# Down-projection weights in 8 KB runs, expert activations with even and odd features apart

## The chip, the core and the metric

The kernel runs on one core of one Trainium2 chip. The metric is the device time of one execution in microseconds (us), as the median of several runs. The core has five instruction streams that matter here: TensorE (PE, the matrix multiplies, with PEld for its weight loads), VectorE (DVE), ScalarE (ACT), GpSimd (POOL) and SyncE (SP, which in this kernel issues nearly all DMA transfers). Sixteen DMA engines carry the transfers between the chip's HBM and the on-chip SBUF.

## What is computed

One decoder layer on 256 tokens of width 1024, in float32: three token mixers (block-sparse attention, short convolution, cross-attention), then a routed feed-forward part with 32 experts, then a final RMSNorm. The change touches the experts alone. Each token goes to its four best experts. Cut to what matters, an expert computes:

```python
def expert_block(args):
    xb, e = args
    gu = xb @ w_gu[e] + b_gu[e]
    g = jnp.minimum(gu[:, :D_EXPERT], SWIGLU_LIMIT)
    lin = jnp.clip(gu[:, D_EXPERT:], -SWIGLU_LIMIT, SWIGLU_LIMIT)
    glu = g * jax.nn.sigmoid(SWIGLU_ALPHA * g)
    return ((lin + 1.0) * glu) @ w_down[e] + b_down[e]
```

`w_gu[e]` is 1024 x 2048 (8 MB), `w_down[e]` is 1024 x 1024 (4 MB). All 32 experts together hold 384 MB of weights, and each weight is read once.

## The kernel before

The kernel has two stages. The first, up to about 300 us, is the mixers: weights come in pieces of 1 MB into a ring of buffers. The second is the experts, one *step* per expert. In a step TensorE multiplies the expert's gathered tokens (64 slots) with `w_gu`, ScalarE and VectorE form the activations, TensorE transposes them and multiplies them with `w_down`, and the result is scattered back into accumulators in PSUM.

Weights of the experts arrive in pieces of 1024 KB (1.0486 MB as the profile counts), all issued by SP, in program order on one queue. `up_piece` (line 333) loads 128 rows of `w_gu` into one of the 16 slots of `ring`: partition p gets row p of the piece, 2048 floats, one run of 8 KB in HBM and in SBUF. Eight such pieces make an expert. `down_piece` (line 343) loads 256 rows of `w_down` into one of the four slots of `dring`: partition p gets rows p and p + 128 of the piece, each 1024 floats, that is two runs of 4 KB that lie 512 KB apart in HBM. Four such pieces make an expert, and `dring` holds just one expert's down weights.

SP waits before an up piece until TensorE has used what was in its slot (`pieces_used`), and before a down piece likewise (`downs_used`). For most of the experts it issues in the order up(e + 2), down(e + 1), up(e + 3), down(e + 2); the last eight experts (`IN_ORDER`) go up(e), down(e), and so the last transfers that TensorE needs are the up pieces of expert 31 and, behind them, its down pieces.

One step on the compute engines:

- TensorE, line 1245: 64 matmuls over the eight up pieces, with a wait for each piece; the gate half goes to `gate_ps` and the linear half to `lin_ps`. The 64 slots fill half of the array's columns, so that the features 0 to 511 sit in partitions 0 to 63 and the features 512 to 1023 in partitions 64 to 127, and `hid` is 128 x 512.
- VectorE, lines 940, 941, 944 and 947: `g_sb` = min(gate, 7), `hid` = clipped linear half, `hid` = (`hid` + 1) * `g_sb`, and last `hid` = `hid` * `sg`, where `sg` is ScalarE's sigmoid of `g_sb` (line 571). The last one sets `hid_ready`.
- TensorE meanwhile transposes the scatter matrix, gathers the next tokens (lines 1253, 1210, 1168), then waits for `hid_ready`, transposes `hid` in four blocks of 128 features (line 1265) into `gate_ps`, and ScalarE copies them to `hidT` (line 576).
- TensorE, line 1281: 32 matmuls with the four down pieces, with a wait for each piece (`down_in`), into `y_ps`. The k-th block of 128 rows is multiplied with the block of `hidT` that holds the same 128 features.

What orders the work is fixed in the code: each engine's program is a loop written by hand with semaphores between the engines.

Of the kernel before, what the change touches and what calls it, by code (L numbers as in the profile page):

```python
# [18 lines left out]
P = 128  # L19
# [95 lines left out]
def build(nc, a, out, scratch, ctx):  # L115
# [4 lines left out]
    ALU = mybir.AluOpType  # L120
# [20 lines left out]
    dring = region("dring", [P, DRING, PIECE])  # L141
# [20 lines left out]
    ident = consts[:, C_ID:C_ID + P]  # L162
# [59 lines left out]
    g_sb = region_r[:, 512:1024]  # L222
    sg = region_r[:, 1024:1536]
    hid = region_r[:, 1536:2048]
    hidT = region_r[:, 3072:3584]

    x2T = region_r[:, 0:2048].rearrange("p (c t) -> p c t", c=KC)
    logit_parts = region_r[:, 4096:4352]
# [19 lines left out]
    gate_ps, lin_ps, tr_ps, y_ps = bank[4], bank[5], bank[6], bank[7]  # L248
# [11 lines left out]
    down_in = [sem(f"down_in{n}") for n in range(DRING)]  # L260
# [23 lines left out]
    g_ready, up_read, hid_half, hid_ready = sem("g_ready"), sem("up_read"), sem("hid_half"), sem("hid_ready")  # L284
# [12 lines left out]
    def _(sp):  # L297
# [11 lines left out]
        p = 0  # L309
# [30 lines left out]
                up_piece(expert, slot0 + c, c)  # L340

        def down_piece(expert, j):
            sp.dma_start(dring[:, j, :].rearrange("p (c n) -> p c n", c=2),  # L343
                         a["w_down"][0, bass.ds(expert, 1), j * 256:(j + 1) * 256, :]
                         .rearrange("e (c p) n -> p (e c) n", p=P)).then_inc(down_in[j], 16)

        def expert_down(expert, uses):

# [34 lines left out]
        with sp.Fori(0, IN_ORDER) as i:  # L383
            for u in range(2):
                e = i * 2 + (e0 + u)
# [210 lines left out]
    def _(dve):  # L596
# [197 lines left out]
        for g in range(len(GROUPS)):  # L794
            p = N_PROJ + 3 * g
            for u in range(2):
                j = ATT_H + 2 * g + u
# [53 lines left out]
        for t in range(TT):  # L851
            last = dve.scalar_tensor_tensor(logit[:, t, :], bank[5][:, t * E:(t + 1) * E], norm[:, 2, 6 + t:7 + t], b_rt,
                                            ALU.mult, ALU.add)
# [7 lines left out]
        for k in range(TOPK):  # L861
            for t in range(TT):
                if k == 0:
                    last = dve.tensor_scalar(mask[:, t, :], slot_no[:, 0:E], best_i[:, t, 0:1], None, ALU.is_equal)
                else:
                    last = dve.scalar_tensor_tensor(mask[:, t, :], slot_no[:, 0:E], best_i[:, t, k:k + 1],
                                                    mask[:, t, :], ALU.is_equal, ALU.add)
# [49 lines left out]
        for t in range(TT):  # L917
            for b in range(PASSES):
                last = dve.tensor_scalar(wexp[:, t, b * E:(b + 1) * E], elog[:, t, :], small[:, 4 + t:5 + t], None, ALU.mult)
        dve.memset(wexp[:, :, STEPS:], 0.0)  # L920
        last = dve.memset(place[:, :, STEPS:], -1.0)
# [11 lines left out]
        with dve.Fori(0, more * (E // 4) + E // 4) as i:  # L933
            for u in range(4):
                s = i * 4 + u
                if u % 2 == 0:
                    dve.wait_ge(gathered, s + 2)
                    gather_matrices(s + 2)
                dve.wait_ge(pieces_used, (s + 1) * KC + N_MIX)
                dve.tensor_scalar(g_sb, gate_ps[:, :], LIMIT, None, ALU.min).then_inc(g_ready, 1)  # L940
                dve.tensor_scalar(hid, lin_ps[:, :], LIMIT, -LIMIT, ALU.min, ALU.max).then_inc(up_read, 1)  # L941
                dve.wait_ge(g_ready, s + 1)
                dve.wait_ge(up_read, s + 2)
                dve.scalar_tensor_tensor(hid, hid, 1.0, g_sb, ALU.add, ALU.mult).then_inc(hid_half, 1)  # L944
                dve.wait_ge(hid_half, s + 1)
                dve.wait_ge(sig_ready, s + 1)
                dve.tensor_tensor(hid, hid, sg, ALU.mult).then_inc(hid_ready, 1)  # L947
                dve.wait_ge(w_slot_ready, s + 1)
                dve.tensor_scalar(scaT[u % 2][:, :, :].rearrange("p t s -> p (t s)"), y_ps[:, 0:TT * P], 0.0, None,
                                  ALU.not_equal).then_inc(scaT_sb, 1)  # L950
                bias_selector(s + 1)
                dve.wait_ge(gathered, s + 3)
                gathered_half(tr_ps, (u // 2 + 1) % 2, u % 2)
                scatter_matrix(s + 1)

                dve.wait_ge(downs_used, (s + 1) * DRING)
                dve.wait_ge(y_high, s + 1)
                dve.scalar_tensor_tensor(y_parts[64:128, 0:512], y_ps[0:64, :], w_slot[0:64, :],  # L958
                                         y_parts[0:64, 0:512].bitcast(fp32), ALU.mult, ALU.subtract)
                dve.scalar_tensor_tensor(y_parts[0:64, 512:1024], y_ps[64:128, :], w_slot[64:128, :],  # L960
                                         y_parts[64:128, 512:1024].bitcast(fp32), ALU.mult, ALU.subtract)\
                    .then_inc(y_ready, 1)
# [3 lines left out]
        for t in range(TT):  # L966
# [6 lines left out]
            for half in range(2):  # L973
                cut = slice(half * 512, half * 512 + 512)
                last = dve.scalar_tensor_tensor(x2[:, t, cut], acc[t][half][:, :], at, gain_out[:, cut], ALU.mult, ALU.mult)
# [4 lines left out]
    def _(pe):  # L980
        mm, transpose = pe.matmul, pe.transpose
# [167 lines left out]
        for j in range(4):  # L1149
# [6 lines left out]
            for n, (k, t, half) in enumerate(order):  # L1156
                c = 2 * j + k
                last = product(bank[2 + 2 * t + half][:, :], (merged_high, merged_low), w,
                                              (slice(None), c, slice(t * P, (t + 1) * P)),
                                              (slice(None), k, slice(half * 512, half * 512 + 512)), c == 0, c == KC - 1)  # L1160
# [18 lines left out]
        for t in range(TT):  # L1179
            pe.wait_ge(x2T_sb if t else x2T_copied, 2)  # L1180
            for c in range(KC):
                at = 32 * (c % 4)
                last = mm(bank[4 - t][at:at + 32, 0:P], w_rt[:, c, :], x2T[:, c, t * P:(t + 1) * P],
                          start=(c < 4), stop=(c >= 4))
            last.then_inc(logit_parts_done, 1)

        for t in range(TT):
            pe.wait_ge(logit_parts_sb, t + 1)
            last = mm(bank[5][:, t * E:(t + 1) * E], logit_parts[:, t * P:(t + 1) * P], pick[:, 0:E], start=True, stop=True)
# [34 lines left out]
        for t in range(TT):  # L1224
            last = transpose(bank[7][0:E, t * P:(t + 1) * P], wexp[:, t, 0:E], ident)
# [6 lines left out]
        with pe.Fori(0, more * (E // 4) + E // 4) as i:  # L1232
            for u in range(4):
                s = i * 4 + u
                slot0 = 8 if u % 2 == 0 else 0

                pe.wait_ge(up_read, s + 1)
                bias_rows(0)
                for c in range(KC):
                    if u % 2 == 0 and c % 4 == 0:  # L1240
                        pe.wait_ge(xg_sb, s + 1 + c // 4)
                    pe.wait_ge(piece_in[slot0 + c], i * 32 + 16 * (u // 2) + 16 * (loads_before(slot0 + c) + 1))
                    for k, ps in enumerate((gate_ps, lin_ps)):
                        for half in range(2):
                            last = mm(ps[64 * half:64 * half + 64, :], xg[u // 2][:, c, 64 * (u % 2):64 * (u % 2) + 64],  # L1245
                                      ring[:, slot0 + c, k * F + half * 512:k * F + half * 512 + 512],
                                      start=False, stop=(c == KC - 1))
                    last.then_inc(pieces_used, 1)

                pe.wait_ge(y_ready, s + 1)  # L1250
                pe.wait_ge(sca_ready, s + 1)
                for t in range(TT):
                    last = transpose(y_ps[:, t * P:(t + 1) * P], sca[:, t, :], ident)
                last.then_inc(scaT_done, 1)

                pe.wait_ge(xg_sb, s + 2)
                if u % 2 == 0:
                    pe.wait_ge(gat_ready, i * 2 + (u // 2 + 2))
                gather(tr_ps, u % 2)
                pe.wait_ge(scaT_sb, s + 1)  # L1260
                scatter((u + 1) % 2, 0, False)

                pe.wait_ge(hid_ready, s + 1)
                for c in range(4):
                    last = transpose(gate_ps[:, c * P:(c + 1) * P], hid[:, c * P:(c + 1) * P], ident)  # L1265
                last.then_inc(hidT_done, 1)
                scatter((u + 1) % 2, 1, False)

                pe.wait_ge(up_read, s + 2)
                pe.wait_ge(sel_ready, s + 2)  # L1270
                bias_rows(1)
                pe.wait_ge(hidT_sb, s + 2)
                pe.wait_ge(scaT_sb, s + 2)
                pe.wait_ge(w_slot_ready, s + 1)
                for c in range(KC):
                    if c % 2 == 0:
                        pe.wait_ge(down_in[c // 2], (s + 1) * 16)
                    lhsT = hidT[:, (c % 4) * P + 64 * (c // 4):(c % 4) * P + 64 * (c // 4) + 64]
                    for half in range(2):
                        at = (c % 2) * D + half * 512  # L1280
                        last = mm(y_ps[64 * half:64 * half + 64, :], lhsT, dring[:, c // 2, at:at + 512],  # L1281
                                  start=(c == 0), stop=(c == KC - 1))
                    if c % 2:
                        last.then_inc(downs_used, 1)
# [45 lines left out]
```

## Time and profile before

| what | before |
|---|---|
| time, median of 3 runs | 1239.49 us (1239.25 to 1241.49) |
| time of the profiled execution | 1238.82 us |
| its span, first to last instruction | 1236.7 us |
| TensorE busy | 1130.2 us, 91% |
| VectorE busy | 387.2 us, 31% |
| ScalarE busy | 263.6 us, 21% |
| bytes moved by DMA | 452.08 MB |

The profiled execution lies 0.67 us below the median of the runs, and 2.1 us of it lie outside the span. A page of the profile shows the span in 40 slices with the busy share of each engine; views of the trace show single stretches: what each engine did, how many bytes the DMA engines moved and in packets of which size, and what an engine waited for. A busy TensorE is not TensorE at its peak, since its matmuls are pipelined and their ends are modelled.

### The profile page before, as it was taken

The page shows a single profiled execution, that of the slowest core. Times are in us where ns is not written, and L with a number is a line of the kernel's source. Part 1 is how long each engine was busy: PE and PEld are TensorE (multiplying, and loading weights), DVE is VectorE, ACT ScalarE, POOL GpSimd, SP SyncE. Part 2 cuts the span into 40 slices and gives each one's busy share as a digit, 9 for nine tenths or more (in the row PEclk, how much of TensorE's full clock was granted, in tenths as well). Part 3 has the DMA queues.
Part 4 walks back from the last instruction along what each step waited for, and adds up shares of the span by engine and source line. Part 5 has one row for each costly group of instructions (what it writes and reads, how often), then busy time and mean ns, then how long its engine had stood idle before and what let it go on. Part 6 is the DMA issues. An engine that isn't in the chain of part 4 may idle for free.

```text
span 1236.7 us, 15845 instructions
## 1 busy us (share of the span) xinstructions
PE 1130.2 (91%) x6083; PEld 583.4 (47%) x6083; DVE 387.2 (31%) x716; ACT 263.6 (21%) x403; POOL 8.3 (1%) x10
## 2 busy tenths in 40 slices
PE   5999999998999999889998889998898999988886
PEld 4999999995443333333333333333333333333332
DVE  6657655564231221212121212122222222221213
ACT  5334575442111110101010101010111111010102
POOL 2000000000000000000000000000000000000000
PEclk8999999999999999999999999999999999999999
DMA  7984344776999999999999999999999999999995
GB/s 261 346 270 160 125 166 140 290 282 250 420 418 417 418 418 418 417 418 417 418 418 418 418 418 418 417 419 417 417 417 417 411 418 418 417 418 418 418 418 224
DMA packets 109427, 452.08 MB, mean 366 GB/s; under 512 B 7074, under 2 KB 38039, under 8 KB 76631
## 3 DMA queue, kind: packets, MB, share of 16 engines
q1 hardware_dynamic: 108871, 449.95, 91.3%
q0 software_dynamic: 528, 1.73, 0.5%
q8 instruction: 21, 0.34, 0.1%
q14 instruction: 7, 0.06, 0.0%
HBM read 450.59 MB, written 1.06 MB: 365 GB/s over the span
## 4 chain that ended last, share of the span: by engine, by line
SPq 40%; PE 38%; DMA 15%; DVE 3%; issue 3%; ACT 0%; DVEq 0%; ACTq 0%
SPq L343 21%; PE bank L991 19%; SPq L333 18%; PE bank L1245 8%; DMA dring<-in_w_down_dram 8%; PE bank L1281 6%; DMA ring<-in_w_gu_dram 6%; DVE region_r L944 1%; DVE region_r L947 1%; DVE region_r L940 1%; PE bank L1265 1%; DVE region_r L941 0%; PE bank L1216 0%; PE bank L998 0%; DVE memT_low L636 0%
## 5 line engine op out<-in xcount | busy, mean ns | idle before, releaser
L1245 PE MATMUL bank<-ring,region_x 128*64 128x512 f32 x2048 | 452.7, 595 | 14.4 <-DMA ring<-in_w_gu_dram 14.4
L1281 PE MATMUL bank<-dring,region_r 128*64 128x512 f32 x1024 | 253.1, 637 | 56.1 <-DMA dring<-in_w_down_dram 55.1
L1245 PEld LDWEIGHTS bank<-ring,region_x 128*64 128x64 f32 x2048 | 141.7, 137 | 305.0 <-issue 263.7
L1281 PEld LDWEIGHTS bank<-dring,region_r 128*64 128x64 f32 x1024 | 71.3, 144 | 223.7 <-DMA dring<-in_w_down_dram 112.3
L940 DVE TENSOR_SCALAR region_r<-bank 128x512 f32<-128x512 f32 x32 | 22.1, 692 | 374.4 <-PE bank L1245 374.4
L958 DVE SCALAR_TENSOR_TENSOR y_parts<-bank,region_r,y_parts 64x512 fp32r<-64x512 f32 x32 | 23.8, 744 | 350.8 <-ACT y_parts L580 350.8
L571 ACT ACTIVATE region_r<-region_r 128x512 f32<-128x512 f32 x32 | 20.2, 630 | 439.3 <-DVE region_r L940 439.3
L991 PE MATMUL bank<-hT_high,w_high 128*128 128x256 f32 x384 | 110.8, 289 | 0.0
L991 PE MATMUL bank<-hT_low,w_high 128*128 128x256 f32 x384 | 108.6, 283 | 0.0
L991 PE MATMUL bank<-hT_high,w_low 128*128 128x256 f32 x384 | 108.6, 283 | 0.0
L646 DVE TENSOR_TENSOR w_low<-ring,w_high 128x2048 fp32r<-128x2048 f32 x39 | 89.2, 2290 | 55.4 <-ACT w_high L436 55.3
L436 ACT ACTIVATE w_high<-ring 128x2048 fp32r<-128x2048 f32 x40 | 76.4, 1912 | 73.3 <-PE bank L991 71.2
L579 ACT ACTIVATE y_parts<-bank,region_r 64x512 fp32r<-64x512 f32 x32 | 21.8, 682 | 312.8 <-PE bank L1281 312.8
L991 PEld LDWEIGHTS bank<-hT_high,w_high 128*128 128x128 f32 x384 | 73.6, 192 | 2.0 <-issue 1.7
L991 PEld LDWEIGHTS bank<-hT_low,w_high 128*128 128x128 f32 x384 | 73.6, 192 | 0.5 <-issue 0.5
L991 PEld LDWEIGHTS bank<-hT_high,w_low 128*128 128x128 f32 x384 | 73.6, 192 | 0.0
L1210 PE MATMUL bank<-region_r,region_h 128*128 128x128 f32 x544 | 66.2, 275 | 1.4 <-DVE region_r L881 1.4
L1210 PEld LDWEIGHTS bank<-region_r,region_h 128*128 128x128 f32 x544 | 63.3, 192 | 1.5 <-issue 1.5
L1168 PE MATMUL bank<-y_parts,scaT 128*128 128x512 f32 x132 | 46.7, 436 | 0.0
L576 ACT ACTIVATE region_r<-bank 128x512 f32<-128x512 f32 x32 | 19.1, 598 | 55.0 <-PE bank L1265 55.0
L1216 PE MATMUL bank<-b_parts,sel 128*128 128x512 f32 x65 | 29.1, 448 | 1.3 <-DVE region_x L887 0.7
L1265 PE MATMUL bank<-consts,region_r 128*128 128x128 f32 x128 | 21.0, 287 | 9.6 <-DVE region_r L947 9.6
(229 smaller groups left out, 907.4 us busy)
## 6 DMA issues: line engine op xcount, KB each, us to landing
ring<-in_w_gu_dram SPq DMA_DIRECT2D x256, 1024.0 KB, 20.3
dring<-in_w_down_dram SPq DMA_DIRECT2D x128, 1024.0 KB, 23.9
ring<-in_w_in_dram SPq DMA_DIRECT2D x26, 1024.0 KB, 9.7
ring<-in_w_mem_kv_dram SPq DMA_DIRECT2D x4, 1024.0 KB, 11.8
ring<-in_w_out_dram SPq DMA_DIRECT2D x4, 1024.0 KB, 4.8
ring<-in_w_br_conv_dram SPq DMA_DIRECT2D x2, 1024.0 KB, 5.1
ring<-in_w_br_att_dram SPq DMA_DIRECT2D x2, 1024.0 KB, 5.2
ring<-in_w_br_xatt_dram SPq DMA_DIRECT2D x2, 1024.0 KB, 5.0
```

Source lines behind the costliest of these rows:

```text
L333: sp.dma_start(ring[:, slot, :], a["w_gu"][0, bass.ds(expert, 1), c * P:(c + 1) * P, :] .rearrange("e p n -> (e p) n")).then_inc(piece_in[ ...
L343: sp.dma_start(dring[:, j, :].rearrange("p (c n) -> p c n", c=2), a["w_down"][0, bass.ds(expert, 1), j * 256:(j + 1) * 256, :] .rearrange( ...
L436: act.activation(w_high[p % 3][:, :], ring[:, q, :], ACT.Copy).then_inc(w_high_ready, 1)
L646: dve.tensor_tensor(w_low[q][:, :], ring[:, q, :], w_high[p % 3][:, :].bitcast(fp32), ALU.subtract)\
L940: dve.tensor_scalar(g_sb, gate_ps[:, :], LIMIT, None, ALU.min).then_inc(g_ready, 1)
L991: ins = mm(dst, lhsT[l][at_l], rhs[r][at_r], start=first and n == 0, stop=last and n == 2)
L1168: last = mm(acc[t][half][:, :], scaT[n][:, t, :], y_parts[:, half * 512:half * 512 + 512], start=False, stop=stop)
L1210: last = mm(ps[:, c * P:(c + 1) * P], h2[:, t, at:at + P], gat[:, t, :], start=(t == 0), stop=(t == TT - 1))
L1216: mm((gate_ps, lin_ps)[k][:, :], sel[:, :], b_parts[:, k * 512:k * 512 + 512], start=True, stop=False)
L1245: last = mm(ps[64 * half:64 * half + 64, :], xg[u // 2][:, c, 64 * (u % 2):64 * (u % 2) + 64], ring[:, slot0 + c, k * F + half * 512:k * F ...
L1265: last = transpose(gate_ps[:, c * P:(c + 1) * P], hid[:, c * P:(c + 1) * P], ident)
L1281: last = mm(y_ps[64 * half:64 * half + 64, :], lhsT, dring[:, c // 2, at:at + 512], start=(c == 0), stop=(c == KC - 1))
```

## The change

Two rows of `w_down` that are neighbours in HBM now go to one partition. Partition p of a down piece gets the rows 2p and 2p + 1 of the piece instead of p and p + 128. In HBM and in SBUF that is one run of 8 KB per partition in place of two of 4 KB; the same bytes, as many transfers, and the same slots.

The block of rows that one matmul sees is then no longer 128 neighbours, but the even or the odd rows of the 256. The activations have to be put in the same order before they are transposed. This is done in the multiply that ends the activations: it reads `hid` and `sg` with a step of two elements (all even features of 256, then all odd ones) and writes them one after the other. It writes into `g_sb` instead of over `hid`, and the four transposes read `g_sb`. The number of instructions, their order on each engine and the waits stay the same.

```diff
+    in_pairs = "p (j q c) -> p j c q"
+    hid_pairs = hid.rearrange(in_pairs, j=2, c=2)
+    sg_pairs = sg.rearrange(in_pairs, j=2, c=2)
+    hid_even_odd = g_sb.rearrange("p (j c q) -> p j c q", j=2, c=2)
...
         def down_piece(expert, j):
-            sp.dma_start(dring[:, j, :].rearrange("p (c n) -> p c n", c=2),
-                         a["w_down"][0, bass.ds(expert, 1), j * 256:(j + 1) * 256, :]
-                         .rearrange("e (c p) n -> p (e c) n", p=P)).then_inc(down_in[j], 16)
+            sp.dma_start(dring[:, j, :], a["w_down"][0, bass.ds(expert, 1), j * 256:(j + 1) * 256, :]
+                         .rearrange("e (p c) n -> p (e c n)", c=2)).then_inc(down_in[j], 16)
...
-                dve.tensor_tensor(hid, hid, sg, ALU.mult).then_inc(hid_ready, 1)
+                dve.tensor_tensor(hid_even_odd, hid_pairs, sg_pairs, ALU.mult).then_inc(hid_ready, 1)
...
-                    last = transpose(gate_ps[:, c * P:(c + 1) * P], hid[:, c * P:(c + 1) * P], ident)
+                    last = transpose(gate_ps[:, c * P:(c + 1) * P], g_sb[:, c * P:(c + 1) * P], ident)
```

## Rows read from the trace of the kernel before

**Rows 1.** The page: span, 40 slices of DMA share and GB/s, packets by size.

```profile
span 1236.7 us, 15845 instructions
...
DMA  7984344776999999999999999999999999999995
GB/s 261 346 270 160 125 166 140 290 282 250 420 418 417 418 418 418 417 418 417 418 418 418 418 418 418 417 419 417 417 417 417 411 418 418 417 418 418 418 418 224
DMA packets 109427, 452.08 MB, mean 366 GB/s; under 512 B 7074, under 2 KB 38039, under 8 KB 76631
```

**Rows 2.** DMA view of 303.5 to 1210 us, the experts: packets, bytes, rate.

```profile
DMA packets 67365, 378.18 MB, mean 417 GB/s; under 512 B 5760, under 2 KB 5760, under 8 KB 36653
```

**Rows 3.** SP's queue: duration of an issue (min/median/max) at lines 343 and 333.

```profile
L343 SPq DMA_DIRECT2D dring<-in_w_down_dram x128: 368/4098/5482, 227.3 to 1198.2; - x128
...
DMA to landing us min/median/max: 6.9/23.9/27.1
...
L333 SPq DMA_DIRECT2D ring<-in_w_gu_dram x256: 328/885/4377, 221.2 to 1185.2; - x128
```

**Rows 4.** Windows: us, busy PE, PEld, DVE, ACT, POOL; PEclk, DMA share, GB/s.

```profile
577.00:594.00 17.00, 16.41 (x76) 5.33 (x75) 2.28 (x7) 2.65 (x3) 0.00 (x0) 1.00 1.01 421
597.00:604.50 7.50, 5.54 (x21) 1.99 (x22) 1.42 (x5) 0.60 (x1) 0.00 (x0) 0.77 1.03 411
607.50:624.00 16.50, 16.20 (x74) 5.20 (x74) 1.50 (x2) 1.36 (x2) 0.00 (x0) 1.00 1.01 422
627.00:634.50 7.50, 5.60 (x19) 1.96 (x21) 1.56 (x5) 0.60 (x1) 0.00 (x0) 0.78 1.03 410
...
958.50:976.50 18.00, 15.45 (x64) 5.01 (x64) 2.88 (x7) 1.96 (x3) 0.00 (x0) 0.91 1.02 399
```

**Rows 5.** DMA view of 607.5:624, 627:634.5 and 34.5:38.5 us, in this order.

```profile
DMA packets 954, 6.96 MB, mean 422 GB/s; under 512 B 105, under 2 KB 105, under 8 KB 105
...
DMA packets 799, 3.08 MB, mean 410 GB/s; under 512 B 48, under 2 KB 48, under 8 KB 799
...
DMA packets 1436, 1.45 MB, mean 364 GB/s; under 512 B 16, under 2 KB 1436, under 8 KB 1436
```

**Rows 6.** TensorE in order of time: start, us, line, count [idle before <- releaser].

```profile
640.21 13.95 PE L1245 MATMUL bank<-ring,region_x 128*64 128x512 f32 x64
...
657.08 0.66 PE L1265 MATMUL bank<-consts,region_r 128*128 128x128 f32 x4 [0.30 <-DVE region_r L947]
...
660.37 1.94 PE L1281 MATMUL bank<-dring,region_r 128*64 128x512 f32 x8 [1.92 <-DMA dring<-in_w_down_dram]
...
668.03 1.94 PE L1281 MATMUL bank<-dring,region_r 128*64 128x512 f32 x8 [0.61 <-DMA dring<-in_w_down_dram]
...
670.33 1.94 PE L1245 MATMUL bank<-ring,region_x 128*64 128x512 f32 x8
```

**Rows 7.** TensorE in order of time, the last step, 1197 to 1224 us.

```profile
1197.69 1.94 PE L1245 MATMUL bank<-ring,region_x 128*64 128x512 f32 x8 [0.31 <-DMA ring<-in_w_gu_dram]
...
1210.12 1.94 PE L1245 MATMUL bank<-ring,region_x 128*64 128x512 f32 x8 [0.56 <-DMA ring<-in_w_gu_dram]
...
1216.40 7.09 PE L1281 MATMUL bank<-dring,region_r 128*64 128x512 f32 x32
```

**Rows 8.** TensorE in order of time, an early step, 324 to 351 us.

```profile
324.80 13.96 PE L1245 MATMUL bank<-ring,region_x 128*64 128x512 f32 x64
...
350.55 13.95 PE L1245 MATMUL bank<-ring,region_x 128*64 128x512 f32 x64
```

**Rows 9.** VectorE's groups of lines 646 and 947: shapes, count | busy us, mean ns.

```profile
L646 DVE TENSOR_TENSOR w_low<-ring,w_high 128x2048 fp32r<-128x2048 f32 x39 | 89.2, 2290 | 55.4 <-ACT w_high L436 55.3
...
L947 DVE TENSOR_TENSOR region_r<-region_r 128x512 f32<-128x512 f32 x32 | 22.1, 692 | 1.1
```

## The prediction

> **What bounds the kernel now.** I read the slices of the page first. From the eleventh on, that is in the whole expert stage, the DMA engines are busy in nine tenths or more of every slice but the last, and the rate is flat at 417 to 418 GB/s [rows 1]. The DMA view of 303.5 to 1210 us says the same over the stage: 378.18 MB at a mean of 417 GB/s [rows 2]. A rate that doesn't move for 900 us while the work on the other engines changes is a limit. The second view is SP's queue. Issuing a transfer takes as little as 0.33 to 0.37 us where the queue is empty, but 4.1 us at the median for a down piece [rows 3]: SP stands in the issue until the queue has room, so the queue is fed ahead of time. Third, TensorE in order of time. In the middle of the stage it waits for the first down piece of a step (1.92 us) and for the fourth (0.61 us) [rows 6], and one step lasts 670.33 - 640.21 = 30.12 us. In an early step, with the buffers still full, the same work takes 350.55 - 324.80 = 25.75 us [rows 8]. So TensorE could be some 4.4 us per step faster than the weights come. In the last step it waits for one up piece after the other [rows 7], and all that follows hangs on the last of them. The end is therefore the landing of the last up piece plus a fixed tail, and that landing is the sum of all pieces queued ahead of it.
>
> **Two rates inside the one.** Pieces flow in the order of issue, so a step has a stretch of up pieces alone and one of down pieces alone. Windows that hold only one kind differ: up pieces flow at 421 and 422 GB/s, down pieces at 411 and 410 [rows 4]. The packets tell what separates them: in an up window all packets but the 105 small ones have 8 KB, in a down window none has [rows 5]. TensorE sees it from outside. Down pieces release it at (668.03 - 660.37) / 3 = 2.553 us from one to the next [rows 6], up pieces at (1210.12 - 1197.69) / 5 = 2.486 us [rows 7]. By the rates, 1.0486 MB / 0.4215 = 2.488 us for an up piece and 1.0486 / 0.4103 = 2.556 us for a down piece; 8 x 2.488 + 4 x 2.556 = 30.13 us, which is the step as seen.
>
> Is it the size of the packet? On one of 16 engines an 8 KB packet takes 16 x 8192 B / 421.5 GB/s = 310.9 ns and a 4 KB packet 159.7 ns. A fixed part f per packet and a part per byte give 2 x 159.7 - 310.9 = f = 8.5 ns. A 1 KB packet would then take (310.9 - 8.5) / 8 + 8.5 = 46.3 ns, 354 GB/s on 16 engines; the mixers' 1 KB packets, which go to another place beside other work, run at 364 GB/s where they are dense [rows 5]. Three sizes on one line is why I take the run length as the cause.
>
> **The change part by part.**
>
> *The transfers.* A down piece becomes a transfer of the same form as an up piece: 128 partitions, one run of 8 KB each. Its packets halve, from 256 to 128, eight fewer on each engine, and it should flow like an up piece: 2.488 us in place of 2.556, 0.068 us less. The pieces that count are those in the saturated stretch ahead of the last up piece: the down pieces of experts 1 to 30, 120 of them (expert 0 is loaded in the mixers, expert 31 behind the last up piece). 120 x 0.068 = 8.2 us. The step becomes 12 x 2.488 = 29.86 us, still 4.1 us over TensorE's own 25.75, so TensorE doesn't become the bound; it waits 0.27 us less per step. The down pieces of expert 31 are not waited for: the last 32 matmuls run without a gap for 7.09 us [rows 7]. Nothing there.
>
> *One stretch apart.* At 958.5 to 976.5 us, where the order of issue changes and the eight down pieces of two experts follow each other, the rate is 399 [rows 4]: SP can refill a slot of `dring` only when TensorE has used it, and the queue nearly runs dry. Against 410 that costs 18 x 11 / 410 = 0.5 us. With faster packets this loss may grow by what those eight pieces gain, 8 x 0.068 = 0.5 us, or vanish, 0.5 us to the good. I take it as it is, 0.
>
> *The multiply.* No row shows VectorE reading with a step of two elements. The same multiply over the same elements takes 692 ns, and 2048 elements take 2290 [rows 9], so an element costs (2290 - 692) / 1536 = 1.04 ns. A gain is excluded: as many elements go through one at a time. Bounds: 0 more, or every element twice, 512 x 1.04 = 533 ns more. I take 0, from the row with the same operation, type and count. In a step in mid-stage either would be hidden: the multiply releases TensorE's transposes [rows 6], and TensorE then stands idle for 1.92 us before the first down piece. In the early steps TensorE has no such gap, but there the DMA engines are busy without it. It shows once, behind the last up piece: 0 to 0.5 us.
> The Trainium skill speaks against this part (Vector Engine (DVE) Microarchitecture Reference, section "Measured stream behaviour on trn2"): a port of VectorE streams at full rate only over pairs of neighbouring words, and two sources stepping word by word cost 1.75 to 2.5 ns per column. By that the multiply takes some 0.4 to 0.75 us more (an estimate from that page), and the sum would be 7.5 to 7.8 us in place of 8.2; no row here shows it.
>
> *The rest.* The transposes read another buffer of the same shape, `g_sb` is free by then (ScalarE's sigmoid, the last reader, releases the multiply) and is next written a step later, behind TensorE's next up matmuls. No wait is added. 0.
>
> The sum is 8.2 us against the profiled execution's 1238.82: 1230.6. The median of the runs lies 0.67 us above that execution, so the forecast is 1231.3.
>
> **The rivals.**
>
> *No gain: the run length doesn't set the rate.* The down windows also differ in what runs beside them (VectorE and the transposes are active, TensorE's granted clock is 0.77 or so [rows 4]) and in where they write. Then the 410 would stay, and the time with it: 1239.5. So also if the queue cut an 8 KB run in two. Against it: the 1 KB packets on the same line, and up pieces of just this form, which do go in 8 KB packets.
> The Trainium skill has this rule (DMA: Bandwidth & Descriptors, section "Specifications"): 512 bytes are enough for line rate. By it 4 and 8 KB would be equal; the 410 against 422 of this trace speaks against that.
>
> *Half the gain.* With packets halved, SP can get further ahead in a queue of limited room and then waits for TensorE to free a slot of `dring`. If such waits empty the queue as at 958.5 to 976.5 in more places, say 0.13 us per step, 30 x 0.13 = 4 us go back: 1235.4. Against it: an up piece's slot was read a whole step before it is refilled, and the queue holds some 8 MB (23.9 us from issue to landing at the median [rows 3]).
>
> *Slower: the multiply becomes the bound.* Its place is between the clipped halves and the transposes, in every step. It decides from the point where TensorE's step passes 29.86 us, that is 4.1 us more on the multiply, and the kernel is slower than before from 4.4 us more, over seven times its 692 ns. At 5.5 us, eight times, the step is 25.75 + 4.8 = 30.55 us and the time 1239.5 + 30 x 0.43 = 1252. Nothing in the trace comes near such a price per element.
>
> **How the numbers follow.** Forecast 0.83, no gain 0.08, half the gain 0.06, slower 0.03. The forecast's own bounds: 0.5 us each way from the stretch apart, 0.5 us less from the multiply, up to 1 us less if the rate of down pieces stays at 420, and the spread of the runs (1239.25 to 1241.49 before). That is 1229.5 to 1233.7; the upper end goes to 1234.5 for part of the half-gain case. Faster means by more than 0.2%, 2.5 us, about what a measurement of this kernel can tell from no change: 0.83 + 0.06 = 0.89. Same 0.08, slower 0.03.
>
> **What would show it.** Right: 16,384 packets fewer in all (93,043) and 32,768 fewer under 8 KB (43,863); 421 to 422 GB/s flat over the expert stage; steps of 29.86 us in mid-stage; the issue of a down piece well below 4.1 us, since it has half the packets to place; TensorE's wait ahead of the first down piece still well over 1 us. Wrong: down windows that stay at 410 although the packets have 8 KB (first rival), dips in the rate beside waits of SP for TensorE (second), or TensorE without a wait for down pieces in mid-stage and a multiply of several us (third).

## The result

| | before | after |
|---|---|---|
| time, median of 4 runs each | 1239.37 us (1239.21 to 1241.49) | 1230.21 us (1228.55 to 1232.04) |
| time of the profiled execution | 1238.82 us | 1228.55 us |
| span | 1236.7 us | 1226.5 us |

The ratio is 0.9923, with a 95% interval of 0.9903 to 0.9942: 0.8% faster, 9.2 us at the medians and 10.3 us between the two profiled executions. Run again later the changed kernel took 1230.35 us (5 runs), a ratio of 0.9933 (0.9920 to 0.9947).

The page of the changed kernel, the lines that answer [rows 1]:

```profile
span 1226.5 us, 15845 instructions
...
DMA  7984354776999999999999999999999999999995
GB/s 260 351 266 160 120 168 151 277 272 258 422 422 421 422 422 422 422 421 422 422 422 422 422 421 422 422 422 422 422 422 422 422 422 423 421 422 422 422 422 224
DMA packets 93042, 452.07 MB, mean 369 GB/s; under 512 B 7074, under 2 KB 38039, under 8 KB 43863
```

The DMA engines are as busy as before and still set the pace, but the flat part stands at 421 to 423 GB/s in place of 417 to 420 with one slice of 411. There are 16,385 packets fewer, and 32,768 fewer under 8 KB, for the same bytes. Windows of the changed kernel (columns as in [rows 4]); down pieces flow in the first, the fourth window holds the eight down pieces in a row that had run at 399:

```profile
624.00:633.00 9.00, 5.84 (x25) 1.45 (x24) 0.26 (x2) 0.00 (x0) 0.00 (x0) 1.00 1.01 421
634.50:652.50 18.00, 17.71 (x89) 6.95 (x85) 4.96 (x11) 3.75 (x6) 0.00 (x0) 1.00 1.01 421
848.00:857.00 9.00, 9.00 (x46) 3.00 (x44) 0.00 (x0) 0.00 (x0) 0.00 (x0) 1.00 1.01 422
953.50:973.00 19.50, 17.45 (x77) 5.34 (x79) 1.50 (x2) 1.36 (x2) 0.00 (x0) 1.00 1.01 421
```

There is one rate now, whichever weights flow. TensorE in order of time, a step in mid-stage, as in [rows 6] (lines of the changed file: 1248 up, 1268 transposes, 1284 down):

```profile
635.63 13.95 PE L1248 MATMUL bank<-ring,region_x 128*64 128x512 f32 x64
...
652.51 0.66 PE L1268 MATMUL bank<-consts,region_r 128*128 128x128 f32 x4 [0.29 <-DVE region_r L950]
652.92 0.71 PE L1171 MATMUL bank<-y_parts,scaT 128*128 128x512 f32 x2
653.47 0.40 PE L1219 MATMUL bank<-b_parts,sel 128*128 128x512 f32 x1
655.70 1.94 PE L1284 MATMUL bank<-dring,region_r 128*64 128x512 f32 x8 [1.83 <-DMA dring<-in_w_down_dram]
...
663.14 1.94 PE L1284 MATMUL bank<-dring,region_r 128*64 128x512 f32 x8 [0.54 <-DMA dring<-in_w_down_dram]
```

Down pieces release TensorE every (663.14 - 655.70) / 3 = 2.480 us (2.553 before), and it waits 1.83 us ahead of the first one (1.92). Counted over the packets (the time in which the 12.58 MB of one expert land, on the mean of the steps in mid-stage), a step is 29.82 us against 30.12. The wait for VectorE ahead of the transposes is 0.29 us as before. SP's queue, as in [rows 3]:

```profile
L347 SPq DMA_DIRECT2D dring<-in_w_down_dram x128: 328/1856/3239, 227.1 to 1183.6; - x128
...
L337 SPq DMA_DIRECT2D ring<-in_w_gu_dram x256: 327/1929/3260, 221.0 to 1173.7; - x128
```

A down piece now takes SP as long to issue as an up piece, 1.86 against 1.93 us at the median, where it had been 4.10 against 0.89. That fits a queue whose room is given out by packets, since both kinds now have as many. VectorE's multiply, as in [rows 9]:

```profile
L950 DVE TENSOR_TENSOR region_r<-region_r 128x512 f32<-128x512 f32 x32 | 22.1, 692 | 1.1
```

### The profile page after: what moved, and what is told of

It is laid out like the page before. It is cut to its first block, busy times and chain, and to the rows that moved or that the text cites. A ratio compares the mean times of both kernels' runs of the same rounds, so it can differ in the third digit from the quotient of the medians.

```text
span 1226.5 us, 15845 instructions
## 1 busy us (share of the span) xinstructions
PE 1119.8 (91%) x6083; PEld 580.7 (47%) x6083; DVE 387.3 (32%) x716; ACT 263.7 (21%) x403; POOL 8.3 (1%) x10
## 4 chain that ended last, share of the span: by engine, by line
PE 44%; DMA 28%; SPq 21%; DVE 4%; issue 2%; ACT 0%; DVEq 0%; ACTq 0%
DMA dring<-in_w_down_dram 21%; PE bank L994 19%; SPq L337 15%; PE bank L1248 12%; PE bank L1284 8%; DMA ring<-in_w_gu_dram 6%; SPq L347 5%; PE bank L1219 1%; DVE region_r L947 1%; DVE region_r L950 1%; DVE region_r L943 1%; PE bank L1268 1%; DVE region_r L944 1%; PE bank L1171 0%; DVE memT_low L639 0%
## 5 line engine op out<-in xcount | busy, mean ns | idle before, releaser
L1284 PE MATMUL bank<-dring,region_r 128*64 128x512 f32 x1024 | 243.5, 614 | 58.1 <-DMA dring<-in_w_down_dram 57.1
## 6 DMA issues: line engine op xcount, KB each, us to landing
dring<-in_w_down_dram SPq DMA_DIRECT2D x128, 1024.0 KB, 25.9
```

## The experiments

My theory was that a packet costs a fixed time on its DMA engine whatever its size, that the weights set the step, and that the multiply is hidden. The rivals were that the place in HBM and not the packet matters, that the multiply has a part in it, and that 422 GB/s is a ceiling. Each kernel's ratio is against the kernel before in the same session.

| kernel | median, us | ratio (95%) | step in mid-stage, us |
|---|---|---|---|
| neighbouring rows, 4 KB packets | 1238.55 | 0.9999 (0.9989 to 1.0009) | 30.12 |
| the multiply alone | 1239.49 | 0.9999 (0.9990 to 1.0009) | 30.12 |
| the transfers alone | 1229.60 | 0.9920 (0.9904 to 0.9937) | 29.83 |
| neighbouring rows, 2 KB packets | 1256.76 | 1.0142 (1.0121 to 1.0163) | 30.73 |
| down pieces in 16 KB runs | 1231.15 | 0.9937 (0.9920 to 0.9954) | 29.67 |
| up pieces in 16 KB runs | 1224.22 | 0.9880 (0.9863 to 0.9896) | 29.52 |
| both in 16 KB runs | 1223.01 | 0.9871 (0.9856 to 0.9886) | 29.37 |
| both, other order of issue | 1219.76 | 0.9845 (0.9828 to 0.9863) | 29.36 |

### Packet or place: neighbouring rows in 4 KB packets

```diff
-            sp.dma_start(dring[:, j, :], a["w_down"][0, bass.ds(expert, 1), j * 256:(j + 1) * 256, :]
-                         .rearrange("e (p c) n -> p (e c n)", c=2)).then_inc(down_in[j], 16)
+            at = j % 2 * D
+            sp.dma_start(dring[:, j // 2 * 2:j // 2 * 2 + 2, at:at + D],
+                         a["w_down"][0, bass.ds(expert, 1), j * 256:(j + 1) * 256, :]
+                         .rearrange("e (p c) n -> p (e c) n", c=2)).then_inc(down_in[j], 16)
```

The down matmuls read their rows from the shared slots accordingly; expert 0's third down piece is issued later, since it now touches the fourth slot.

> Neighbouring rows in 4 KB packets: HBM is read as in the changed kernel (rows 2p and 2p + 1 to partition p), and the activations are in its order, but the two rows of a partition land in two slots that two pieces share, so that a packet has 4 KB again. Theory (a fixed cost per packet): down pieces at about 2.56 us, steps of 30.12 us, 1239.4 us as the kernel before. Rival (what helps is that a piece is read from neighbouring places in HBM): steps of 29.82 us, 1230.2 us.

It took 1238.55 us, no different from the kernel before. The packets on its page, and two windows, first up pieces, then down pieces:

```profile
DMA packets 109426, 452.07 MB, mean 366 GB/s; under 512 B 7074, under 2 KB 38039, under 8 KB 76631
```

```profile
607.50:624.00 16.50, 16.50 (x80) 5.77 (x77) 2.17 (x4) 1.37 (x2) 0.00 (x0) 1.00 1.01 421
627.00:634.50 7.50, 5.57 (x19) 1.38 (x17) 0.79 (x3) 0.50 (x1) 0.00 (x0) 0.77 1.03 411
```

All of the change but the 8 KB packet is in this kernel: a piece comes from the same places in HBM, partition p gets neighbouring rows, the multiply sets the features apart. The packets are back at the old number, the down windows at 411 GB/s, and the gain is gone. The 4 KB packets land in other places of `dring` here than in the kernel before, at the same rate, so the place in SBUF isn't it either. It was the packet.

### One part at a time

The multiply alone is the kernel before with this edit:

```diff
-                dve.tensor_tensor(hid, hid, sg, ALU.mult).then_inc(hid_ready, 1)
+                dve.tensor_tensor(hid_even_odd, hid_pairs, sg_pairs, ALU.mult).then_inc(hid_ready, 1)
...
-                    last = transpose(gate_ps[:, c * P:(c + 1) * P], hid[:, c * P:(c + 1) * P], ident)
+                    last = transpose(gate_ps[:, c * P:(c + 1) * P], g_sb[:, c * P:(c + 1) * P], ident)
```

> The multiply alone: the kernel before with the multiply that reads in steps of two and writes even and odd features apart; the transfers stay in two 4 KB runs, so the rows of w_down meet the wrong features in this kernel. Theory (the multiply costs nothing, 692 ns as before): 1239.4 us. Rival (reading in steps of two costs, or the new order gains something by itself): a multiply of 1.05 to 1.43 us, still hidden but for up to 0.7 us at the end, 1240; or below 1237.

The transfers alone are the changed kernel with `dve.tensor_tensor(g_sb, hid, sg, ALU.mult)`.

> The transfers alone: the changed kernel with a multiply that reads and writes in one row, so the features are not set apart and meet the wrong rows in this kernel. Theory (the transfers are the whole gain): 1230.2 us, steps of 29.82 us. Rival (part of the gain is the multiply's): above 1233.

The multiply alone took 1239.49 us (ratio 0.9999) and lasted 692 ns at the median; the transfers alone took 1229.60 us (0.9920). The gain is the transfers' to within the intervals.

### Does the cost follow the number of packets: 2 KB and 16 KB

For 2 KB a row is cut in two halves, which two pieces interleave in their shared slots:

```diff
+            pair = dring[:, j // 2 * 2:j // 2 * 2 + 2, :].rearrange("p c (h b n) -> p c h b n", h=2, b=2)
+            sp.dma_start(pair[:, :, :, j % 2, :],
+                         a["w_down"][0, bass.ds(expert, 1), j * 256:(j + 1) * 256, :]
+                         .rearrange("e (p c) (h n) -> p (e c) h n", c=2, h=2)).then_inc(down_in[j], 16)
```

> Neighbouring rows in runs of 2 KB: as the 4 KB kernel, with half a row per packet, 512 packets in a down piece. Theory (a fixed cost of 9.3 ns per packet): 32 packets on each engine in place of 8, 24 x 9.3 ns = 0.22 us more per down piece than in the changed kernel, steps of 30.71 us, 120 x 0.22 = 27 us: 1257 us. Rival (what was gained lies between 4 and 8 KB alone, a matter of the row's boundary): as with 4 KB, 1239 us.

It took 1256.76 us. For 16 KB the down pieces are 2 MB, two per expert:

```diff
+            sp.dma_start(dring[:, 2 * j:2 * j + 2, :].rearrange("p s n -> p (s n)"),
+                         a["w_down"][0, bass.ds(expert, 1), j * 512:(j + 1) * 512, :]
+                         .rearrange("e (p c) n -> p (e c n)", c=4)).then_inc(down_in[j], 16)
...
+    hid_pairs = hid.rearrange("p (q c) -> p c q", c=4)
```

> Four neighbouring rows per partition, one 16 KB run, down pieces of 2 MB, two per expert; the multiply sets the features apart by four. Theory (a fixed cost of 9.3 ns per packet): eight packets fewer on each engine per 2 MB, 0.075 us on each of the 60 transfers that count, 4.5 us in all: steps of 29.68 us, 1225.7 us, up to 1 us more because the slots of the down weights come free in larger pieces. Rival (422 GB/s is the limit of the path whatever the run): steps of 29.82 us, 1230.2 to 1231 us.

The steps came out as the theory has them, 29.67 us, but the time did not: 1231.15 us, no better than the changed kernel and just above the 1230.2 to 1231 us that the rival gave. The steps tell the two apart, since the rival had them at 29.82 us. Two windows and SP's queue where two experts' down pieces follow each other:

```profile
955.00:965.00 10.00, 8.57 (x37) 2.65 (x39) 0.00 (x0) 1.20 (x2) 0.00 (x0) 1.00 0.80 303
965.00:975.00 10.00, 10.00 (x50) 3.40 (x48) 1.50 (x2) 0.17 (x1) 0.00 (x0) 1.00 0.99 406
```

```profile
931.11 33.01 SPq L346 DMA_DIRECT2D dring<-in_w_down_dram  x4
```

A slot now comes free only when TensorE has used 2 MB of it, SP is held for 33 us over four transfers, and the rate falls to 303 GB/s for 10 us. Counted over packets the steps there took 32.32 and 30.06 us in place of 29.67, 3.0 us lost. I had allowed 1 us. Against the profile of the changed kernel its stage also began 0.9 us later and its first step took 0.7 us more, as varies between runs, and the tail behind the last up piece is 1.3 us longer; together that is 5.9 us, more than the 4.5 us gained (the two profiled executions differ by 1.6 us).

The up pieces in 16 KB runs load two slots at once. The copy that scales the tokens' features writes them apart in pairs, and the norm gains stand in the same order:

```diff
+            for c in range(0, KC, 2):
+                slot = slot0 + c
+                sp.wait_ge(pieces_used, uses + c + 1)
+                sp.dma_start(ring[:, slot:slot + 2, :].rearrange("p s n -> p (s n)"),
+                             a["w_gu"][0, bass.ds(expert, 1), c * P:(c + 2) * P, :]
+                             .rearrange("e (p k) n -> p (e k n)", k=2)).then_inc(piece_in[slot], 16)
...
+            act.activation(h2[:, t, :].rearrange("p (j k q) -> p j k q", j=4, k=2), x2[:, t, :].rearrange("p (j q k) -> p j k q", j=4, k=2),
+                           ACT.Copy, scale=norm[:, 2, 6 + t:7 + t]).then_inc(h2_sb, 1)
```

> The up pieces of experts 2 to 31 in pairs, two neighbouring rows of w_gu per partition, one 16 KB run of 2 MB; the tokens' features are set apart in the same way by the copy that scales them. Down pieces as in the changed kernel. Theory (9.3 ns per packet): 8 packets fewer on each engine for each of 120 pairs, 0.075 us each, 9 us; steps of 29.52 us; 1.7 us are lost at the end, because TensorE begins on the last 2 MB when all of it has landed: 1223 us. Rival (the path is at its limit with 8 KB): 1232 us.

It took 1224.22 us, 1.2 us more than forecast, and the steps are 29.52 us as forecast. Against the profile of the changed kernel the stage begins 1.9 us later, and the tail behind the last up piece is 2.7 us longer, where I had put 1.7. The DMA view of 400 to 900 us, one line per kernel: 2 KB, the kernel before, the changed kernel, 16 KB down, 16 KB up, and both in 16 KB (a kernel that comes further below):

```profile
DMA packets 52714, 204.86 MB, mean 410 GB/s; under 512 B 3132, under 2 KB 3132, under 8 KB 35900
```

```profile
DMA packets 37054, 208.88 MB, mean 418 GB/s; under 512 B 3184, under 2 KB 3184, under 8 KB 19932
```

```profile
DMA packets 28976, 210.98 MB, mean 422 GB/s; under 512 B 3223, under 2 KB 3223, under 8 KB 3223
```

```profile
DMA packets 24218, 212.03 MB, mean 424 GB/s; under 512 B 2689, under 2 KB 2689, under 8 KB 2689
```

```profile
DMA packets 19523, 213.13 MB, mean 426 GB/s; under 512 B 2163, under 2 KB 2163, under 8 KB 2163
```

```profile
DMA packets 14708, 214.23 MB, mean 428 GB/s; under 512 B 1633, under 2 KB 1633, under 8 KB 1633
```

In the same 500 us the bytes rise as the packets fall. By the step, per packet on one engine: from 8 to 4 KB (30.12 - 29.82) / 32 = 9.4 ns, from 8 to 2 KB (30.73 - 29.82) / 96 = 9.5 ns, from 8 to 16 KB down 0.15 / 16 = 9.4 ns, up 0.30 / 32 = 9.4 ns. The steps are read to 0.01 us, and the changed kernel's was 29.83 in a repeat; 0.01 us is 0.6 ns in the third of these figures and 0.3 ns or less in the others. Within that, four changes of size in two streams give one price. The ceiling at 422 falls.

### How much the cover holds: a longer way to the multiply

One VectorE instruction more ahead of the multiply, with n = 4 and n = 9:

```diff
+                dve.tensor_reduce(region_r[:, 3840:3840 + n], consts[:, 0:512].unsqueeze(1).broadcast_to([P, n, 512]),
+                                  AX.X, ALU.max)
```

> The changed kernel with one more VectorE instruction ahead of the multiply, a maximum over 4 x 512 elements whose result nobody reads: some 2.2 us more between the clipped halves and the transposes in every step. Theory (TensorE has 4.1 us per step to spare, the weights set the step): steps stay at 29.82 us and the 2.2 us show once, at the end: 1232.4 us. Rival (the chain from the gate to the transposes sets part of the step): 30 x 2.2 = 66 us, 1296 us.

> As the kernel with 4 x 512, with 9 x 512 elements: some 4.9 us more per step, past the 4.1 us. Theory: TensorE now sets the step, 25.75 + 4.9 = 30.65 us from the first expert on; the last up matmuls start at about 299 + 31 x 30.65 = 1249 us of the span and the end is 14 + 24.7 + 4.9 us behind that, 1293 us of span, 1295 us. Rival (the cover is larger than 4.1 us): the weights still set the step, 1235 us.

Both missed. With n = 4 (2.29 us) the steps in mid-stage stayed at 29.83 us, as the theory has it, but the one run took 1242.15 us. TensorE in order of time, from the last wait for weights to the last step:

```profile
967.40 1.94 PE L1286 MATMUL bank<-dring,region_r 128*64 128x512 f32 x8 [0.53 <-DMA dring<-in_w_down_dram]
...
969.69 13.95 PE L1250 MATMUL bank<-ring,region_x 128*64 128x512 f32 x64
...
1199.20 13.95 PE L1250 MATMUL bank<-ring,region_x 128*64 128x512 f32 x64
```

The same steps in the changed kernel:

```profile
963.66 13.95 PE L1248 MATMUL bank<-ring,region_x 128*64 128x512 f32 x64
...
1066.64 8.80 PE L1248 MATMUL bank<-ring,region_x 128*64 128x512 f32 x40
...
1183.80 5.61 PE L1248 MATMUL bank<-ring,region_x 128*64 128x512 f32 x24
```

From 969.69 us on, the eight steps to 1199.20 take 28.69 us each and TensorE waits for no weights: in the last part it sets the time. In the changed kernel the same eight steps go from 963.66 to 1183.80 us, 27.5 us each, because the first four of them run without a wait for weights at TensorE's own 25.75 us: the change of order has left it behind the weights. On the mean only 27.5 - 25.75 = 1.8 us per step are to spare there, and the 2.29 us don't fit. They alone would make the step 28.04 us; four of the eight take 27.93 or 27.94 us, and the other four 29.3 to 29.5, with the granted clock at a mix of its two levels behind the wait (0.81 at 986 to 995 us against 1.00 at 1045 to 1055).

That is 9.4 us of the 13.5 by which this span is longer. TensorE was 6.0 us late already at 969.69 us: 1.3 us by a later start of the stage (300.18 against 298.84 us), the rest by the first steps. There the buffers are full and TensorE sets its own pace (up to 640 us it waits for no weights), now 27.94 to 29.64 us a step in place of 25.75, so SP gets slots later, and the queue runs short in the first of them. The window of 320 to 335 us in this kernel and in the changed one:

```profile
320.00:335.00 15.00, 15.00 (x63) 5.03 (x64) 2.32 (x5) 1.96 (x3) 0.00 (x0) 0.90 0.94 354
```

```profile
320.00:335.00 15.00, 15.00 (x71) 4.95 (x69) 1.50 (x2) 1.36 (x2) 0.00 (x0) 1.00 1.02 423
```

Behind 1199.20 us some 2 us come back, since the last step no longer waits for weights. With n = 9 (4.95 us) the one run took 1352.66 us. TensorE waits for VectorE in every step, and behind the wait it runs slowly:

```profile
646.23 1.11 PE L1270 MATMUL bank<-consts,region_r 128*128 128x128 f32 x4 [5.16 <-DVE region_r L952]
646.99 1.20 PE L1173 MATMUL bank<-y_parts,scaT 128*128 128x512 f32 x2
647.99 0.63 PE L1221 MATMUL bank<-b_parts,sel 128*128 128x512 f32 x1
```

The same groups take 0.66, 0.71 and 0.40 us in the changed kernel. The windows (columns as in [rows 4]) of a step of this kernel and of one of the changed kernel:

```profile
605.00:638.00 33.00, 27.84 (x128) 11.07 (x124) 11.41 (x16) 4.35 (x7) 0.00 (x0) 0.90 0.92 372
```

```profile
605.00:635.00 30.00, 26.20 (x128) 9.77 (x124) 5.81 (x11) 3.07 (x6) 0.00 (x0) 1.00 1.02 423
```

The granted clock is 0.90 of full speed against 1.00, a mix of the levels of 1.2 and 2.4 GHz: after the wait TensorE runs at the lower one for a while. I had left that out: steps of 31.86 us (656.35 - 624.49) and of 32.99 us take turns, (1304.88 - 300.16) / 31 = 32.41 us on the mean of the stage, not 30.65. That TensorE sets the pace past the cover is shown; the price was mis-sized.

### Both streams, and the place where the queue runs dry

> Both in 16 KB runs: the up pieces in pairs as in the kernel with up pieces of 16 KB (1224.2 us), the down pieces in 2 MB as in the kernel with down pieces of 16 KB. Theory (a fixed cost per packet, and a price for slots that come free 2 MB at a time): steps of 29.37 us, 4.5 us less than the up pieces alone over 30 experts; against it the 3.0 us that the 2 MB down pieces lost where two experts' down pieces follow each other, and 0.4 us of the slower multiply: 1223 us. Rival (the gain per packet ends with both streams at 16 KB): 1226 us or more, steps of 29.52 us.

It took 1223.01 us, as forecast, with steps of 29.37 us and one of 33.91 us, where the two experts' down pieces follow each other. The last kernel takes that place away by its order of issue (the experts behind it go on as up(e), down(e)):

```diff
+        expert_up(e0, 8, ups + e0 * KC, (0, 2))
         expert_down(e0 - 1, downs + DRING * (e0 - 1))
+        expert_up(e0, 8, ups + e0 * KC, (4, 6))
+        expert_down(e0, downs + e0 * DRING)
...
```

> Both streams in 16 KB runs, and the first expert of the last eight is issued in another order: down(22), half of up(24), down(23), the other half, down(24), and so on, so that no two experts' down pieces follow each other. Theory (in the kernel with both streams at 16 KB the queue ran dry there, 4.5 us over a step of 29.37): that loss goes, 1223.0 - 4.5 = 1218.5 us, a median of 1217.5 to 1220. Rival (the loss moves to the next place where slots come free too late): 1222 us or more.

The window of 950 to 960 us in the kernel with both streams at 16 KB and in the last one, then the page of the last one:

```profile
950.00:960.00 10.00, 10.00 (x41) 3.05 (x39) 0.90 (x2) 1.36 (x2) 0.00 (x0) 0.89 0.64 236
```

```profile
950.00:960.00 10.00, 8.75 (x41) 2.59 (x37) 1.39 (x2) 1.36 (x2) 0.00 (x0) 1.00 1.01 429
```

```profile
span 1217.2 us, 15094 instructions
...
GB/s 264 350 266 147 131 157 168 247 249 274 419 428 426 430 429 428 428 429 429 428 428 429 429 428 428 429 429 428 428 429 429 427 418 429 428 429 429 429 428 198
DMA packets 66543, 452.06 MB, mean 371 GB/s; under 512 B 4119, under 2 KB 35092, under 8 KB 40916
```

It took 1219.76 us, ratio 0.9845 (0.9828 to 0.9863): 20 us less than the kernel before in the same session, and 10 less than the changed one in its sessions. The step of 33.91 us is one of 30.22, so 3.7 of the 4.5 us came back; a smaller dip is left, the slice of 418 GB/s. The changed kernel, run beside the kernel with both streams, repeated its time.

> The changed kernel again, beside the kernel with both streams at 16 KB on one chip. Both theories: 1230.2 us, between 1228.5 and 1232 as in its first runs; steps of 29.82 us.

## Why the prediction was right, point by point

**What bounds the kernel: right.** The step followed the packets' time in every kernel that changed the transfers, and the multiply alone moved nothing.

**The price of a packet: right in kind, 10% too small.** I had f = 8.5 ns and 0.068 us per piece; the runs give 9.4 to 9.5 ns and (30.12 - 29.82) / 4 = 0.075 us. The term of the sum that was mis-sized is this price, because I took it as the small difference of two rates that [rows 4] give in whole GB/s. With 409 GB/s for the down pieces in place of 410.3 a piece takes 2.564 us, and 0.076 us less is the answer. The 7.5 us windows that I chose hold some 750 packets, so that three packets more or fewer at their ends are enough for that. My check by the step, 30.13 against 30.12 us, couldn't show it: turned round, it gives (30.12 - 8 x 2.488) / 4 - 2.488 = 0.066 us, and 0.001 us in the up piece moves that by 0.003.

The third size on my line was also weaker than I wrote. With 9.4 ns a 1 KB packet would take (310.9 - 9.4) / 8 + 9.4 = 47.1 ns, 348 GB/s, and [rows 5] have 364. Those packets go elsewhere, beside other work, and no run here changes their size; the price is shown for 2 to 16 KB.

**The sum.** 120 x 0.075 = 9.0 us, not 8.2. Of the 1.1 us by which the forecast is too high, 0.8 are this. The last up piece of the changed kernel:

```profile
1199.90 1.94 PE L1248 MATMUL bank<-ring,region_x 128*64 128x512 f32 x8 [0.55 <-DMA ring<-in_w_gu_dram]
```

To the 10.2 us between the last up pieces' arrivals in the two profiled executions (1210.12 in [rows 7], 1199.90 after) belong, beside the 9.0, by the packets' counts, 0.4 us at the stretch apart, which vanished; 0.4 us in the stage's first step; and 0.3 us by which the stage began earlier. The last two vary from run to run (the first step took 30.00 us in this profile and 30.39 in the repeat), and the medians differ by 9.2 us; runs that spread over 2 to 3.5 us can't tell 9.0 from 9.4. The tail was fixed, as I had it: 1236.7 - 1210.12 and 1226.5 - 1199.90 are both 26.6 us.

**The stretch apart: within its bounds.** I took it as unchanged, between 0.5 us lost and 0.5 us won. It was won: 421 GB/s where 399 had stood. The executions profiled with 4 KB packets lose 0.3 to 1.1 us there (the kernel before, neighbouring rows in 4 KB, the multiply alone), those with 8 KB nothing (the changed kernel, its repeat, the transfers alone). Why is not shown; it fits that a down piece now stands 25.9 us between issue and landing, where it was 23.9 [rows 3], so that SP is further ahead. The kernels with 2 MB down pieces show the danger that I had named for 8 KB there: 3.0 and 4.5 us lost.

**The multiply: right.** 692 ns, from the row with the same operation. The Trainium skill (Vector Engine (DVE) Microarchitecture Reference, "Measured stream behaviour on trn2") would have it 0.4 to 0.75 us longer; at a step of two elements the trace disagrees, 692 ns. At a step of four, in the kernel with 16 KB down runs, its rule is seen:

```profile
L947 DVE TENSOR_TENSOR region_r<-region_r 128x512 f32<-128x512 f32 x32 | 34.2, 1070 | 1.1
```

That is (1070 - 692) / 512 = 0.74 ns per element more, 1.78 ns per column with the 1.04 of [rows 9], and within that page's 1.75 to 2.5. The steps that cost start between two and four elements.

**The cover: right in mid-stage, too large as a statement on the stage.** I wrote that TensorE has 4.1 us per step to spare. It has in mid-stage; behind the change of order near 964 us it has 1.8 on the mean, and in the first steps, where I had the DMA engines busy without it, 2.29 us more were enough to bring the rate to 354 GB/s for a while. An addition of 2.29 us cost 12 us. The 0.5 us that I had as the multiply's upper bound would have fitted behind the change of order: the last kernel's multiply takes 0.38 us more than 692 ns, and its steps stay at 29.4 us to the end.

**The rivals.** *No gain* fell with the 4 KB kernel, which differs from the changed one in the packet and in the slots it lands in, and with it the rule from the Trainium skill (DMA: Bandwidth & Descriptors, "Specifications") that 512 bytes are enough for line rate: 2, 4, 8 and 16 KB give four rates here. *Half the gain* did not come, but its mechanism is real: it is what the kernel with 16 KB down runs fell to, with larger slots. (The 8 MB that I gave for the queue should have been 10: 23.9 us at 417 GB/s.) *Slower* was kept off by the price of the multiply; its mechanism was shown with 4.95 us more, at a far higher price than the one I gave, 1352.66 us against 1252 for a like addition. My 1252 had two faults. It charged 30 steps with what they exceed 30.12 us, but TensorE's steps in the kernel before last 28.86 us on the mean of the stage, (1193.73 - 299.05) / 31 from the first up matmul to that of the last step, since eight of them run at 25.75; from there, 30.55 us in every step costs 31 x 1.69 = 52 us and not 13. And it left out the clock: steps of 32.41 us in place of 25.75 + 4.95 = 30.70 are another 53 us.

## What to carry to other kernels

In this kernel, where the DMA engines are busy throughout, a packet of 2 to 16 KB costs some 9.4 ns on its engine beside its bytes, and longer runs per partition gain that back: 0.8% from 4 to 8 KB on a third of the bytes, 1.3% with 16 KB on all, and 1.6% with the order of issue changed too. The order of a contraction is free as long as both operands have it, so runs can be made longer by putting neighbouring rows on one partition and permuting the small operand in an instruction that is there anyway. Larger transfers also free their buffers in larger steps: look for the place where the queue can't be refilled ahead, and change the order of issue there.

## What the runs showed of the hardware

- SP's time in an issue measured the room in the queue, not the work of issuing: with half the packets a down piece went from 4.10 to 1.86 us, and an up piece, unchanged itself, from 0.89 to 1.93; with all weights in 16 KB runs both took 0.33 us.
- VectorE read two sources with a step of two elements in the time of a step of one (692 ns over 512 columns), and with a step of four in 1070 ns.
- A wait of 5.16 us per step was followed by matmuls at about half speed (1.20 in place of 0.71 us for the same two); behind a wait of 2.49 us they took 0.70 us in some steps and 1.20 in others.
